# Which engine makes the lower weight parts while VectorE translates the routing's positions

## The reference, cut to what matters

```python
def peer(xn, w_q, sub_keys, u, v):
    q = (xt @ w_q).reshape(T, PEER_HEADS, 2, PEER_HALF)
    s = jnp.einsum('thpc,hpnc->thpn', q, sub_keys).astype(jnp.float32)
    s1, i1 = lax.top_k(s[:, :, 0], PEER_TOPK)
    s2, i2 = lax.top_k(s[:, :, 1], PEER_TOPK)
    cand = (s1[..., :, None] + s2[..., None, :]).reshape(T, PEER_HEADS, PEER_TOPK * PEER_TOPK)
    cidx = (i1[..., :, None] * PEER_N_KEYS + i2[..., None, :]).reshape(T, PEER_HEADS, PEER_TOPK * PEER_TOPK)
    top_s, top_j = lax.top_k(cand, PEER_TOPK)
    expert = jnp.take_along_axis(cidx, top_j, axis=-1)
    gate = jax.nn.softmax(top_s, axis=-1).astype(xn.dtype)
    ...
        h = jax.nn.gelu(jnp.einsum('cd,chkd->chk', xc, u[ec]), approximate=False)
        return jnp.einsum('chk,chkd->cd', gc * h, v[ec])
```

## Time and profile before

| | us |
|---|---|
| median of 3 runs | 3196.53 |
| lowest and highest of them | 3193.64, 3198.44 |
| span of the profiled execution | 3193.6 |
| TensorE busy | 3150.6 |
| VectorE busy | 2545.1 |
| ScalarE busy | 1636.8 |
| GpSimd busy | 1020.8 |
| GpSimd's subtractions, 106 | 263.3 |
| VectorE's subtractions of the same kind, 434 | 530.0 |

### The profile page before, as it was taken

How to read it: one execution, slowest core, us unless ns; L and a number is a source line. 1 busy time by engine, 2 the same in 40 slices (tenths; PEclk the granted TensorE clock), 3 DMA queues, 4 the chain that set the end, 5 groups by cost and what they waited for, 6 DMA issues and landing times.

```text
span 3193.6 us, 48756 instructions
## 1 busy us (share of the span) xinstructions
PE 3150.6 (99%) x17822; PEld 2817.2 (88%) x17822; DVE 2545.1 (80%) x5378; ACT 1636.8 (51%) x3053; POOL 1020.8 (32%) x626
## 2 busy tenths in 40 slices
PE   8999999999999999999999989999999999999999
PEld 7878899999998888888978868899999998888887
DVE  5685898989857988885378876898989866888886
ACT  5343249696943333335255654248686853333333
POOL 1001464545422444520000000354445432444440
PEclk9999999999999999999999999999999999999999
DMA  5123269898999999993222214259898998999994
GB/s 199 44 66 118 85 222 349 308 351 303 354 366 340 379 391 390 396 367 115 68 86 74 87 61 138 81 171 337 314 346 312 345 383 315 374 401 398 389 392 146
DMA packets 324925, 827.33 MB, mean 259 GB/s; under 512 B 26064, under 2 KB 158672, under 8 KB 317520
## 3 DMA queue, kind: packets, MB, share of 16 engines
q1 hardware_dynamic: 250960, 555.75, 48.5%
q0 software_dynamic: 73728, 268.47, 22.5%
HBM read 718.16 MB, written 105.96 MB: 258 GB/s over the span
## 4 chain that ended last, share of the span: by engine, by line
PE 43%; DVE 3%; DMA 2%; ACT 1%; issue 1%; SPq 0%; DVEq 0%; ACTq 0%
PE p_bank L2346 16%; PE p1r_h_ps L2282 16%; PE ba_bank L416 6%; PE o_bank L1753 1%; DMA hiddens<-p_h_sb 1%; PE p1r_gate_ps L2330 1%; PE ba_oT_ps L476 1%; PE ba_t_ps L497 1%; PE p1r_s_ps L2306 0%; PE ba_s_ps L439 0%; DVE p_grow L2711 0%; DVE ba_e L644 0%; ACT p1r_cols L2452 0%; PE ba_s_ps L444 0%; DMA raw<-in_u 0%
## 5 line engine op out<-in xcount | busy, mean ns | idle before, releaser
L2413 ACT ACTIVATE peer_hi<-raw 128x1024 fp32r<-128x1024 f32 x540 | 570.9, 1057 | 673.9 <-PE p_bank L2346 604.3
L2703 DVE TENSOR_TENSOR peer_lo<-raw,peer_hi 128x1024 fp32r<-128x1024 f32 x434 | 530.0, 1223 | 308.1 <-ACT peer_hi L2413 307.3
L2244 POOL TENSOR_TENSOR peer_lo<-raw,peer_hi 128x1024 fp32r<-128x1024 f32 x106 | 263.3, 2485 | 1083.2 <-ACT peer_hi L2413 1083.1
L2256 POOL DMA_INDIRECT p_grow<-in_v_rows,p_expert x256 | 388.6, 1518 | 468.9 <-DVE p_acc L2720 384.1
L2256 POOL DMA_INDIRECT p_grow<-in_u_rows,p_expert x256 | 359.2, 1403 | 506.8 <-DVE p_hid L2711 479.2
L2346 PE MATMUL p_bank<-peer_hi,p_w_hi 128*128 128x512 f32 x1500 | 461.8, 389 | 0.0
L2346 PE MATMUL p_bank<-peer_hi,p_w_lo 128*128 128x512 f32 x1500 | 461.8, 389 | 0.0
L2346 PE MATMUL p_bank<-peer_lo,p_w_hi 128*128 128x512 f32 x1500 | 461.7, 389 | 0.0
L2282 PE MATMUL p1r_h_ps<-h_hi,peer_hi 128*128 128x384 f32 (+2 forms) x1152 | 396.9, 345 | 1.3 <-ACT p_h_sb L2431 0.9
L2282 PE MATMUL p0r_h_ps<-h_hi,peer_hi 128*128 128x384 f32 (+2 forms) x1152 | 396.7, 344 | 0.6 <-DVE peer_lo L2703 0.5
L2282 PE MATMUL p1r_h_ps<-h_lo,peer_hi 128*128 128x384 f32 (+2 forms) x1152 | 391.4, 340 | 0.0
(11 more groups left out here) (438 smaller groups left out, 5531.9 us busy)
## 6 DMA issues: line engine op xcount, KB each, us to landing
raw<-in_u SPq DMA_DIRECT2D x256, 512.0 KB, 6.1
raw<-in_v SPq DMA_DIRECT2D x256, 512.0 KB, 8.3
p_g_sb<-gates SPq DMA_DIRECT2D x64, 768.0 KB, 11.1
hiddens<-p_h_sb SPq DMA_DIRECT2D x240, 192.0 KB, 4.7
p_w_raw<-hiddens SPq DMA_DIRECT2D x60, 768.0 KB, 7.5
gates<-x SPq DMA_DIRECT2D x24, 1024.0 KB, 9.7
raw<-in_w_b_mix SPq DMA_DIRECT2D x38, 512.0 KB, 3.5
raw<-in_w_peer_q SPq DMA_DIRECT2D x32, 512.0 KB, 3.6
```

Source lines behind the costliest of these rows:

```text
L2244: pool.tensor_tensor(lo[:, m % NH, :], raw[:, m % NR, :], hi[:, m % NH, :].bitcast(F32), ALU.subtract).then_inc(lo_pool, 1)
L2256: pool.indirect_dma_start(out=grow[:, g % RG, :], out_offset=None, in_=table, in_offset=bass.IndirectOffsetOnAxis(ap=expert[:, at:at + 1], ...
L2413: act.activation(hi[:, n % NH, :], raw[:, n % NR, :], ACT.Copy).then_inc(hi_ready, 1)
L2703: dve.tensor_tensor(lo[:, m % NH, :], raw[:, m % NR, :], hi[:, m % NH, :].bitcast(F32), ALU.subtract).then_inc(lo_dve, 1)
```

## The change

The change leaves GpSimd the subtraction in the three sorting steps of each routing and gives VectorE those in the six translating steps. It also brings the first condition, for the steps up to the end of the first routing, to the same border.

```diff
     in_route = {s + i for s in route_step for i in range(ROUTE_PIECES)}
...
+    SORTED_PIECES = 3
+
+    in_route = {s + i for s in route_step for i in range(SORTED_PIECES)}
 
     def by_pool(m):
 
-        return m >= READY and (m - 2 <= LIST_END + ROUTE_PIECES or m - 2 in in_route)
+        return m >= READY and (m - 2 < LIST_END + SORTED_PIECES or m - 2 in in_route)
```

More of the change, by code:

```diff
@@ L2049, in peer_stage @@
     hidden_step = {rows_step(PART * (i + 1)): i for i in range(PAIRS // PART)}
-    in_route = {s + i for s in route_step for i in range(ROUTE_PIECES)}
+    SORTED_PIECES = 3
+    in_route = {s + i for s in route_step for i in range(SORTED_PIECES)}
     def by_pool(m):
-        return m >= READY and (m - 2 <= LIST_END + ROUTE_PIECES or m - 2 in in_route)
+        return m >= READY and (m - 2 < LIST_END + SORTED_PIECES or m - 2 in in_route)
     pool_los = [0]
```

## The result

The changed kernel takes 3203.25 us (median, 3195.32 to 3208.14) where the kernel before takes 3196.53 in as many executions: ratio 1.0017, 95% interval 1.0010 to 1.0024. Against the bound of 0.2% that is "no change", and the median lies 0.25 us over the top of the range given (3191 to 3203). The forecast was +0.2 us where +6.7 came between these two medians, +5.4 by the ratio. What the change does to VectorE was forecast rightly; most of the time went elsewhere.

What follows compares the result with a forecast made beforehand. TensorE, nearly always in matmuls, was taken to bound the kernel. Removed waits of -0.8 and +1.0 us in the third routings gave +0.2 us on the median 3196.53: 3196.7, range 3191 to 3203.

Steps and rivals of the forecast that it cites:

- What bounds the kernel: Whole kernel: TensorE has matmuls under way 3150.6 of 3193.6 us; its waits for lower parts are 0.5 and 0.3 us.
- The stretches are GpSimd's doing: Translating steps: GpSimd's subtractions lengthen VectorE instructions running beside them by about 2.2 us each, 8.7 us in one routing.
- the first of the rivals: Translating steps: VectorE's slow instructions have another cause, so lower parts come 7 to 11.5 us late; about 3270, chance 0.04.
- The walk of the third routing: Third routing, translating steps: VectorE makes block 67's lower part 0.5 us late in each layer, adding 1.0 us.
- No cost in the first, second and fourth, and the two old waits go: Other routings: no lower part late, 0 us; TensorE's lower-part waits of 0.5 and 0.3 us vanish, -0.8 us.
- Edits with a price of nothing: SyncE's loads and GpSimd's fetches: loads stay covered, fetches go earlier but held by VectorE's buffer use; 0 us.
- covered by 2 us: Third routing: block 71's load lands at 619.1 after a median 6.1 us, its upper part wanted at about 621.2.
- The third routing is more late than walked, in the milder form: Rival, third routing: one more 2.2 us stretch in each layer, +4.4, 3201; counted within the 0.88 for no change.

Runs made afterwards that it cites:

- the paced ones: Changed kernel plus a GpSimd wait for the step's upper part before fetching in translating steps, run twice: 3199.61 us (ratio 1.0002) and 3201.64 us (1.0011).

## Why the prediction was right in its verdict and short in its sum

Point by point, by its own steps:

- **What bounds the kernel.** Right. There was no microsecond to gain, and a kernel could only lose by making something late. But it read only TensorE's waits for lower parts. The other thing that TensorE waits for is ScalarE, and ScalarE waits for loads and stores, 35.9 and 23.2 us in the kernel before; what room these have was asked for the loads alone, by their median.
- **The stretches are GpSimd's doing.** Right, and shown: all sixteen L2630 at 1.22 us, the first of the rivals (3270) gone, and in the kernel with the first two routings only the third's at 3.31 again. Of what the Trainium skill's page "Perfetto Trace Analysis", section "Optimizing Scalar/DVE Operations", weighs against each other, its second half holds here: VectorE took over 46 subtractions and came out 41 us less busy. It had been put at 53 added and 70 removed, 17 less. By the rows it is 57.4 added (587.4 for 530.0) and so 98.6 removed, which is 2.1 for each of the 46 subtractions: the removed part was under-counted. It took four stretches a routing from the third, and that routing has a fifth: the eight products of L2634 at 605.00 last 3.90 us, beside GpSimd's subtraction of 605.66, where those at 617.48 last 1.71. The walk had them at 1.71 without that stretch and so is not touched by it.
- **The walk of the third routing.** Right: 0.5 us late a layer forecast, 0.76 to 0.78 seen in the changed kernel, 0.70 to 0.72 in the paced ones, and 1.0 us a layer in the stretches of both paced kernels (52.6 for 51.6). In the prediction's sum that is +1.0 and should have been +2.0; 0.3 us a layer have no wait that names them.
- **No cost in the first, second and fourth, and the two old waits go.** Right when paced: 51.7 to 52.1 in the fourth routing where the kernel before has 52.2 and 52.4, so there 0.3 to 0.65 us a layer are saved against this one execution, and the two waits of the earlier trace rows that were to go went. How much of the 0.8 us is the change's is not shown: with the fourth routing unchanged, in the kernel with the first two routings only, they were 0.2 in sum and the stretches 52.1 and 52.1. In the changed kernel itself the fourth costs 1.2 and 1.4 more than before, by the bursts.
- **"Edits with a price of nothing".** This is the step that failed. GpSimd's fetches "go earlier, held by VectorE's use of the buffers as before": they were not held by that before. Six buffers allow five or six fetches at once, and what had kept them apart were the subtractions with their waits for ScalarE. The load of a block was then called "covered by 2 us" over a median of 6.1, and beside a burst it took 11.3 and 13.8; the stores of results had no line at all, and a store is what ended the wait each time that the burst reached TensorE. Taking the bursts away took 3.6 us out of the two fourth routings and up to 2.6 out of a third, which is the larger part of the 5.2 us (by the ratio) between forecast and result.
- **The third routing is more late than walked, in the milder form** (3201). It came, in a smaller size than the bursts: in sixteen profiled third routings with VectorE as the maker and GpSimd in the sorting steps, VectorE had 2.0 us of additional lag once and 1.1 once, and the stretch was longer by about that (54.68 for 52.64; 53.72 for 52.74). The rival named "a landing of a block at the long end" as well, but put its cost on VectorE and nothing in the fourth routing. It came through SyncE's transfers and ScalarE, and in the fourth above all.

The terms as the stretches give them, against the kernel before: the two third routings +2.0 (forecast +1.0), the two fourth routings -0.6 and -1.2 when paced (forecast -0.8), the bursts +3.6 in every profile and 2.6 more in one, additional lag 2.0 in one. In the changed kernel's first profile this gives 2.0 - 0.9 + 3.6 + 2.0 = 6.7 for the 6.6 seen.

That the verdict of no change held owes something to luck. The cost that was put at nothing happened to stay under 6.4 us; nothing in the prediction bounded it, and the interval of the result reaches 1.0024.

What stays open: whether the transfers are late because a burst's packets stand ahead of theirs or only because the 16 engines share their time, since the runs vary the burst and not the queue; why a burst of five in the third routing cost 2.6 us in one of six profiled third routings and nothing that can be told in the others; and where the rest of VectorE's lag in single executions comes from, beyond the stretched row that the timeline shows.

## What to carry to other kernels

An instruction that leaves an engine takes its wait along. When work is moved off an engine that also issues transfers, look at what then stands between the transfers, and count how many can go out at once by the buffers alone. If they had been spaced by the work, keep the wait and drop only the work; one line did that here. And ask for room not only of the engine that bounds the kernel, but of the transfers that hold the ones it waits for, stores out of a ring of two buffers as much as loads: a load whose median is covered by 2 us is covered only as long as the traffic stays as it was.

## What the runs showed of the hardware that was not expected

- A burst of six indirect fetches of 0.52 MB, issued within 8 us, made loads of 512 KB issued in its midst and just after it land 11.3 and 13.8 us after issue instead of 6.1, and stores of 192 KB after 9.3 us in the median instead of 4.1. ScalarE waited 43 to 51 us for such stores in the three profiles with the changed kernel's bursts, 20 to 33 in the nine without bursts in the third and fourth routing.
- VectorE can do 46 subtractions more and be 41 us less busy. One of GpSimd's subtractions of 2.4 us costs VectorE some 2.2 us when it meets one of the instructions at L2616, L2628, L2634 and L2641 (L2634 at 605.00), which is more than the 1.16 us that VectorE needs for the subtraction itself. The sorting instructions don't suffer: the 64 MAX8 (L2589), 64 FIND_INDEX8 (L2593) and 64 MATCH_REPLACE8 (L2594) of the kernel before all take 0.25 to 0.28 us, with GpSimd subtracting in these steps.
- The time of twelve blocks around a routing repeats to 0.04 us between the two paced kernels in the third routing (52.65, 52.62, 52.66, 52.62), while the whole kernel spreads over 9 us and more. Where the whole can't tell two kernels apart, such a stretch can, within limits: the fourth routings of the same two kernels lie up to 0.4 us apart (51.65 to 52.07), and single executions had 2.0 and 2.6 us more in the third.
